# Layer norms taken by token chunk, with the units before and after them reordered chunk by chunk

## The reference

```python
def _layer_norm(x, g, b):
    mu = jnp.mean(xf, axis=-1, keepdims=True)
    var = jnp.mean(jnp.square(xf - mu), axis=-1, keepdims=True)
    return (xf - mu) * lax.rsqrt(var + LN_EPS) * g + b
...
for l in range(DEPTH):
    if l < N_A:
        y, h = _short_conv(x, conv_hist[l], a_w_in[l], a_conv_w[l], a_w_out[l])
    else:
        k_new, v_new, logf_new = _shared_kv(x, kv_w, f_w, f_b)
        cum = lax.cumsum(logf_all, axis=1)
        y = _fox_prompt(...) or _fox_sample(...)
    x = _layer_norm(ALPHA * x + y, ln_g[l, 0], ln_b[l, 0])
    x = _layer_norm(ALPHA * x + _swiglu(x, ffn_w_gu[l], ffn_w_down[l]), ln_g[l, 1], ln_b[l, 1])
```

## Time and profile before

| what | us |
|---|---|
| median of 3 runs (lowest, highest) | 2905.06 (2899.21, 2907.32) |
| the profiled execution | 2906.83 |
| its span, first to last instruction | 2905.2 |
| PE busy | 2696.3 |
| DVE, ACT, POOL busy | 1109.6, 784.1, 951.4 |
| granted PE clock, mean | 0.955 |

### The profile page before, as it was taken

One profiled execution on the slowest core, in us unless ns is written; L12 is line 12 of the kernel. 1 busy time (PEld: TensorE's weight loads), 2 busy tenths in 40 slices (PEclk: granted clock), 3 DMA queues, 4 the chain that ended last, 5 costly groups with the idle time before them and its releaser, 6 DMA issues.

```text
span 2905.2 us, 44679 instructions
## 1 busy us (share of the span) xinstructions
PE 2696.3 (93%) x16907; PEld 2605.1 (90%) x16907; DVE 1109.6 (38%) x2082; ACT 784.1 (27%) x1431; POOL 951.4 (33%) x546
## 2 busy tenths in 40 slices
PE   8999969999999999689997899889799999999994
PEld 8999959999999999579996778779599999999993
DVE  3222362422222222762354555552642222222237
ACT  2111134111111111252223555551511111111114
POOL 2212143112111122352323878843512212112114
PEclk9999969999999999899998989989899999999997
DMA  3111101111111111024688555631011111111111
GB/s 111 44 51 43 45 22 37 47 49 44 45 44 44 53 50 44 23 80 144 197 286 270 143 168 152 179 111 44 22 44 52 44 52 45 44 52 45 44 37 59
DMA packets 203054, 225.87 MB, mean 78 GB/s; under 512 B 13223, under 2 KB 168871, under 8 KB 201884
## 3 DMA queue, kind: packets, MB, share of 16 engines
q1 hardware_dynamic: 194748, 190.40, 21.5%
q0 software_dynamic: 8160, 33.30, 3.7%
HBM read 182.43 MB, written 41.26 MB: 77 GB/s over the span
## 4 chain that ended last, share of the span: by engine, by line
PE 79%; DVE 7%; POOL 4%; issue 4%; DMA 3%; ACT 2%; SPq 1%; POOLq 0%; DVEq 0%; ACTq 0%
PE ps L1746 24%; PE ps L1747 24%; PE ps L1748 24%; POOL ss L830 2%; PE ps L2012 2%; DVE ln_t L1405 1%; DVE ln_t L1409 1%; PE ps L2042 1%; DVE ln_d L1350 1%; PE ps L1997 1%; PE ps L1994 1%; DMA ncb<-ccum 1%; DMA o_t<-oe 1%; PE ps L2029 1%; PE ps L2028 1%
## 5 line engine op out<-in xcount | busy, mean ns | idle before, releaser
L1746 PE MATMUL ps<-xh,whi 128*128 128x344 f32 x3288 | 1068.0, 325 | 31.5 <-POOL xl L711 18.4
L1747 PE MATMUL ps<-xl,whi 128*128 128x344 f32 x3288 | 1055.2, 321 | 0.0
L1748 PE MATMUL ps<-xh,wlo 128*128 128x344 f32 x3288 | 1055.0, 321 | 0.0
L664 POOL TENSOR_TENSOR wlo<-wraw,whi 128x1024 fp32r<-128x1024 f32 x197 | 471.2, 2397 | 1659.0 <-ACT whi L890 1658.9
L1746 PEld LDWEIGHTS ps<-xh,whi 128*128 128x128 f32 x3288 | 620.7, 189 | 59.5 <-POOL xl L711 34.6
L1748 PEld LDWEIGHTS ps<-xh,wlo 128*128 128x128 f32 x3288 | 622.3, 189 | 0.0
L1747 PEld LDWEIGHTS ps<-xl,whi 128*128 128x128 f32 x3288 | 622.1, 189 | 0.0
L890 ACT ACTIVATE whi<-wraw 128x1024 fp32r<-128x1024 f32 x197 | 208.2, 1058 | 1116.9 <-DMA wraw<-ffn_w_gu 649.3
L1746 PE MATMUL ps<-zh,whi 128*128 128x344 f32 x1440 | 465.7, 323 | 17.6 <-DVE x L1477 9.4
L1747 PE MATMUL ps<-zl,whi 128*128 128x344 f32 x1440 | 464.1, 322 | 0.0
L1748 PE MATMUL ps<-zh,wlo 128*128 128x344 f32 x1440 | 462.1, 321 | 0.0
(11 more groups left out here) (209 smaller groups left out, 2384.3 us busy)
## 6 DMA issues: line engine op xcount, KB each, us to landing
wraw<-ffn_w_gu SPq DMA_DIRECT2D x88, 512.0 KB, 3.9
wraw<-ffn_w_down SPq DMA_DIRECT2D x44, 512.0 KB, 3.5
kp<-cache_k SPq DMA_DIRECT2D x32, 512.0 KB, 5.5
vp<-cache_v SPq DMA_DIRECT2D x32, 512.0 KB, 4.1
wraw<-a_w_in SPq DMA_DIRECT2D x24, 512.0 KB, 3.7
wraw<-kv_w SPq DMA_DIRECT2D x16, 512.0 KB, 4.3
q_t<-hl POOLq DMA_DIRECT2D x8, 1024.0 KB, 4.6
v_t<-vst POOLq DMA_DIRECT2D x8, 1024.0 KB, 6.9
```

The lines of the kernel that those rows point to most:

```text
L664: pool.tensor_tensor(narrow(wlo[:, s, :], cols), narrow(wraw[:, s, :], cols), f32(narrow(whi[:, s, :], cols)), ALU.subtract).then_inc(w_lo, 1)
L1746: pe.matmul(out, w_h, m_h, start=start, stop=False)
L1747: pe.matmul(out, w_h, m_l, start=False, stop=False)
L1748: return pe.matmul(out, w_l, m_h, start=False, stop=stop)
```

## The change

The norm is split into steps for one chunk each (`ln_block_mean`, `ln_spread`, `ln_rstd`, `ln_scale` on DVE; `ln_square_sum`, `ln_mean`, `ln_root`, `ln_out` on ACT; `ln_mean`, `ln_var`, `ln_bc` on PE; `ln_low` and `ln_sum` with a chunk on POOL), and the units around it are reordered. The last three of the 8 out- or o-units (`CUT` = 5) run as a `triple`: chunk by chunk, in each chunk the three units, each unit now with a PSUM bank of its own. The first three units behind norms 0 and 2 (gate, up, gate of the FFN) are a triple too, and so are `f`, the first v-unit and the first q-unit behind norm 1. The last group of the down-projection goes over its 24 pieces chunk by chunk. PE's matmuls of the norm are placed between the chunks. The first v-unit's weights get a fourth place (`xraw`, `xhi`, `xlo`). Behind norm 1, ACT takes the chunks of v and q before it starts the decay chain, and DVE takes f and the low part of q likewise. At the end, output rows 0 and 1 are made inside norm 3, and of the last chunk POOL makes three blocks and DVE five. Buffers of the norm move, `ln_mu` becomes two chunks, and the variances go to columns 400 on of a bank that is in use otherwise. The number of matmuls stays the same.

```diff
+CUT = 5
...
+class Pieces:
...
+    def __init__(self, whole, by_chunk):
+        order = [(m, None) for m in whole if m] + [(m, c) for c in range(NCH) for m in by_chunk if m]
+        self.taken = {p: i + 1 for i, p in enumerate(order)}
...
+AFTER_PROJ = Pieces(range(CUT), range(CUT, KB))
+AFTER_DOWN = Pieces((), range(KB))
+LN_PIECES = (AFTER_PROJ, AFTER_DOWN) * DEPTH
+LN_MEAN = ((3, 4, 5), (0, 0, 7)) * DEPTH
+LN_VAR = ((6, 6, 6), (1, 1, 7)) * DEPTH
+LN_BC = ((3, 4, 5), (2, 3, 6)) * DEPTH
+VCOL = 400
...
-                for q in range(4):
-                    gate_up(n0 + q - q % 2, n0 + q - q % 2, q // 2, q % 2, used(g0 + q))
+                for q in range(3):
+                    gate_up(n0 + q - q % 2, n0 + q - q % 2, q // 2, q % 2, (full[q], g0))
+                gate_up(n0 + 2, n0 + 2, 1, 1, (full[0], g0 + 3))
...
             def proj_low(stage, i):
-                for m in range(KB):
-                    low(SLOTS[stage] + m + WR, SLOTS[stage] + m + WR)
-                    if i == 2 and m >= 1:
+                n = SLOTS[stage]
+                for m in range(CUT):
+                    low(n + m + WR, n + m + WR)
+                    if i == 2 and m >= 2:
                         ln_sum(i, m)
-                    if i == 0 and m >= 6:
-                        ln_sum(i, m - 4)
                 if i == 0:
-                    for m in range(4, KB):
+                    for m in range(2, CUT):
                         ln_sum(i, m)
-                ln_low(i)
...
+                for c in range(2):
+                    for m in range(CUT, KB):
+                        ln_sum(i, m, c)
+                ln_sum(i, 5, 2)
+                ln_low(i, 0, 0, 2)
+                ln_sum(i, 6, 2)
+                ln_low(i, 0, 2, 5)
+                low(n + KB, n + KB)
+                ln_sum(i, 7, 2)
+                ln_low(i, 0, 5, 8)
+                low(n + KB + 1, n + KB + 1)
+                low(n + KB + 2, n + KB + 2)
+                for c in range(1, NCH):
+                    ln_low(i, c, 0, KB)
...
                 n0, g0 = SLOTS[stage], UNITS[stage]
-                for m in range(KB):
+                for m in range(CUT):
                     high(n0 + m + WR, n0 + m + WR, (full[2], g0 + m + 1))
                     if i == 2 and m >= 1:
                         ln_squares(i, m)
-                    if i == 0 and m >= 4:
-                        ln_squares(i, m - 3)
                 if i == 0:
-                    for m in range(5, KB):
+                    for m in range(1, CUT):
                         ln_squares(i, m)
+                n, freed = n0 + KB, g0 + KB
+                for m in range(CUT, KB):
+                    ln_squares(i, m, 0)
+                ln_square_sum(i, 0)
+                ln_squares(i, 5, 1)
+                ln_mean(i, 0)
+                ln_squares(i, 6, 1)
+                ln_root(i, 0)
+                ln_squares(i, 7, 1)
+                ln_square_sum(i, 1)
+                ln_squares(i, 5, 2)
+                ln_mean(i, 1)
+                ln_out(i, 0, 0, 2)
+                ln_squares(i, 6, 2)
+                ln_root(i, 1)
+                ln_out(i, 0, 2, 5)
+                high(n, n, (full[0], freed))
+                ln_squares(i, 7, 2)
+                ln_square_sum(i, 2)
+                ln_out(i, 0, 5, 8)
...
+                first_gate(0)
+                ln_out(i, 1, 0, 3)
+                ln_mean(i, 2)
+                ln_out(i, 1, 3, 5)
+                ln_root(i, 2)
+                ln_out(i, 1, 5, 8)
+                first_hidden(0)
+                second_gate(0)
+                ln_out(i, 2, 0, 4)
+                first_gate(1)
+                ln_out(i, 2, 4, 8)
+                first_hidden(1)
+                second_gate(1)
+                first_gate(2)
+                high(n0 + 3, n0 + 3, (full[0], g0 + 3))
+                first_hidden(2)
+                high(n0 + 4, n0 + 4, (full[1], g0 + 3))
+                second_gate(2)
                 high(n0 + 5, n0 + 5, (full[2], g0 + 3))
...
+            high(n0 + 1, n0 + 1, ffn[0].at("down", FG * KB * NCH))
+            ln_out(1, 1, 0, 4)
+            ln_mean(1, 2)
+            ln_out(1, 1, 4, 8)
+            first_v(0)
+            ln_root(1, 2)
+            first_q(0)
+            ln_out(1, 2, 0, 8)
+            for c in range(1, NCH):
+                first_v(c)
+                first_q(c)
+            act.wait_ge(free[1], UNITS["f"] + NCH)
+            act.activation(scol[:, 0, 0, :], stage[0][:, TP:T], ACT.Copy).then_inc(kv["v"], 1)
+            high(n0 + 2, n0 + 2, (full[0], g0 + 2))
+            act.wait_ge(free[0], UNITS["f"] + NCH)
             act.activation(fe[:, :], fz[:, :], ACT.Abs).then_inc(kv["fa"], 1)
...
+            def ln_spread(i, c):
+                s = ln[i]
+                dve.wait_ge(*s.at("mu", c + 1))
+                dve.tensor_tensor(sl(ln_v, c), sl(ln_mp, c), ln_mu[:, c % 2, :], ALU.subtract).then_inc(s["dev"], 1)
+                dve.wait_ge(*s.at("s2", s.pieces.total(KB - 1, c)))
+                dve.wait_ge(*s.at("m2", c + 1))
+                dve.scalar_tensor_tensor(sl(ln_m2, c), sl(ln_m2, c), -1.0 / KB, sl(ln_s2, c), ALU.mult, ALU.add).then_inc(s["dsum0"], 1)
+                dve.wait_ge(*s.at("dsum0", c + 1))
+                dve.wait_ge(*s.at("v2", c + 1))
+                dve.tensor_tensor(sl(ln_m2, c), sl(ln_m2, c), sl(ln_v, c), ALU.add).then_inc(s["dsum"], 1)
...
+            def ln_scale(i, c, blocks):
+                s = ln[i]
+                for k, m in enumerate(blocks):
+                    j = c * KB + (k if i == 3 and c == 2 else m)
                     if j >= 3:
                         dve.wait_ge(*s.at("y", j - 2))
-                    dve.tensor_tensor(ln_t[:, j % 3, :], sl(x32[:, m, :], c), sl(ln_mu, c), ALU.subtract).then_inc(s["t"], 1)
+                    dve.tensor_tensor(ln_t[:, j % 3, :], sl(x32[:, m, :], c), ln_mu[:, c % 2, :], ALU.subtract).then_inc(s["t"], 1)
                     if m == 0:
-                        dve.wait_ge(*s.at("bc", c + 1))
+                        dve.wait_ge(*(s.at("mu", NCH + 1) if i == 3 and c == 2 else s.at("bc", c + 1)))
...
+                def take(m, c):
+                    u = m - CUT
+                    xm = sl(x32[:, m, :], c)
+                    dve.wait_ge(full[u], g0 + CUT + c + 1)
+                    if first:
+                        if m == KB - 1 and c == 0:
+                            dve.wait_ge(stored, 16 * 3)
+                        dve.scalar_tensor_tensor(xm, f32(sl(xh[:, m, :], c)), ALPHA, ps[:, u, 0:CH],
+                                                 ALU.mult, ALU.add).then_inc(free[u], 1)
+                        dve.wait_ge(free[u], g0 + CUT + c + 1)
+                        dve.scalar_tensor_tensor(xm, f32(sl(xl[:, m, :], c)), ALPHA, xm,
+                                                 ALU.mult, ALU.add).then_inc(s["r"], 1)
+                        ln_diff(i, m, c, s.at("r", NCH * CUT + (KB - CUT) * c + u + 1))
+                    else:
+                        dve.tensor_tensor(xm, xm, ps[:, u, 0:CH], ALU.add).then_inc(free[u], 1)
+                        ln_diff(i, m, c, (free[u], g0 + CUT + c + 1))
+                for m in range(CUT, KB):
+                    take(m, 0)
+                ln_block_mean(i, 0)
+                take(5, 1)
+                ln_spread(i, 0)
+                take(6, 1)
+                ln_rstd(i, 0)
+                take(7, 1)
+                ln_block_mean(i, 1)
+                take(5, 2)
+                ln_spread(i, 1)
+                ln_scale(i, 0, range(0, 2))
+                take(6, 2)
+                ln_rstd(i, 1)
+                ln_scale(i, 0, range(2, 5))
+                take(7, 2)
+                ln_block_mean(i, 2)
+                ln_scale(i, 0, range(5, 8))
             proj("out", 0, True)
-            ln_finish(0)
...
+                def last_down(grp):
...
+                    def take(c, a, b):
+                        for m in range(a, b):
+                            j = c * KB + m
+                            down_sum(grp, m, c, j)
+                            if m >= 1:
+                                ln_diff(i, m, c, s.at("sum", DBANKS + grp * KB * NCH + j + 1))
+                    take(0, 0, 8)
+                    ln_block_mean(i, 0)
+                    take(1, 0, 3)
+                    ln_spread(i, 0)
+                    take(1, 3, 5)
+                    ln_rstd(i, 0)
+                    take(1, 5, 8)
+                    ln_block_mean(i, 1)
+                    take(2, 0, 1)
+                    ln_scale(i, 0, range(0, 2))
+                    take(2, 1, 2)
+                    ln_scale(i, 0, range(2, 4))
+                    take(2, 2, 3)
+                    ln_spread(i, 1)
+                    ln_scale(i, 0, range(4, 6))
+                    take(2, 3, 4)
+                    ln_scale(i, 0, range(6, 8))
+                    take(2, 4, 5)
+                    ln_rstd(i, 1)
+                    take(2, 5, 8)
```

(79 more changed lines are left out.)

578 lines of the change are left out of this document (344 added, 234 removed).

## The result

| | median us (lowest, highest) | ratio to before, 95% interval |
|---|---|---|
| before | 2904.6 (2899.21, 2914.52) | |
| changed | 2892.01 (2884.33, 2896.27) | 0.995 [0.9938, 0.9961] |

What follows compares the result with a forecast made beforehand. The prediction took PE's matmuls plus its waits as the bound, paced around the norms by DVE with POOL. Gains at norms 0, 1, 2, 3 less clock, 33.6 + 11 + 23 + 4.4 - 9 = 63, gave 2842 us, range 2795 to 2880.

Steps and rivals of the forecast that it cites:

- The signs on PE's stops: Norms 0 and 2: no PE idle row over 10 us; first FFN unit: PE waits 5 to 9 us for chunk 0's blocks.
- the differences 3 and 4 at t = 14: Norm 0, counted from 353.07: DVE's whole-width differences 3 and 4 with their sums end at 14, between 12 and 16.5.
- 18 us, plus 1.5: Norm 0: DVE's remaining list behind (2, 5) takes 18 us, plus 1.5 for POOL's weight part; chunk 0 out at about 54.
- DVE's next chunk needs 12.5 to 15.5 and its last 10.3, both inside that: Norm 0 behind chunk 0: DVE's work for the later chunks fits inside PE's 36 us.
- 11 to 12 us a chunk: Norm 1, last down-projection: DVE's pace for pieces of 1.53 to 1.9 us; third block mean about 52.5 us after first sum.
- the decay chain: Behind norm 1: chain of 21 us starts after the last q chunk; PE waits some 10 us, next unit 26.2 after the triple.
- my lower bounds: Lowest gains: 20 us at norm 0, 12 at norm 2, 0 at norm 1 and -6 at norm 3.
- I charged 3 us at three norms: Norms 0, 1 and 2: cost of half-clock matmuls after PE's wait, each 24 costing 3.8 us more; 0 to 20 in all.
- Rival B: DVE as the bound throughout: lower bounds, 26 to 40 us gained, 2865 to 2880; chance 0.2.
- rival A: Placement fits: differences not held by the lock, chain hidden behind a unit; upper bounds, 2790 to 2820; chance 0.22.
- Rival C: Slower through PE's clock: short waits keep it at 0.50 through the triples; eight triple units make 2933; chance 0.05.
- D: No effect: DVE's same in-order chain only moves and PE waits elsewhere as long; 2897 to 2913; chance 0.03.

Runs made afterwards that it cites:

- e1: Against the changed kernel, POOL's sums of squares cut to 8 columns per chunk at all four norms (variances wrong): 2873.0 us, 0.9874 of before.
- e2: Against the changed kernel, chunk 1's broadcast and chunk 2's mean moved inside the first FFN chunk at norms 0 and 2: 2886.1 us, 0.9933 of before.
- e13: Against the changed kernel, low parts of the first three FFN units' weights written by ACT instead of POOL at norms 0 and 2: 2892.0 us, 0.9949 of before.
- e11: Against the changed kernel, four more 344-column DVE operations behind each block mean of each norm: 2922.3 us, 1.0047 of before.
- e9: Against the changed kernel, 42 added matmuls ahead of PE's waits for the first FFN unit's weights at norms 0 and 2: 2893.6 us, 0.9956 of before.
- e5: Against the changed kernel, DVE takes chunk 0 of unit 5 ahead of differences 3 and 4 at norm 0: 2892.4 us, 0.9952 of before.
- e6: Against the changed kernel, chunk 1's variances at norms 1 and 3 put into PSUM bank 7 instead of bank 1: 2892.3 us, 0.9952 of before.
- e14: Against the changed kernel, POOL's sums cut to 8 columns, chunk 1's broadcast earlier and three weights' low parts on ACT, together: 2862.7 us, 0.9842 of before.
- e10: Against the changed kernel, POOL's sums cut to 8 columns and the normalised blocks' low parts written by ACT as copies: 2874.5 us, 0.9892 of before.
- e15: Against the changed kernel, the square root's table loaded ahead by an added root one square earlier in ACT's order: 2890.2 us, 0.9941 of before.
- e8_fill: Against the changed kernel, 56 added matmuls behind the wait for weights, just ahead of the first FFN chunk of norms 0 and 2: 2918.2 us, 1.0049 of before.

## Why the prediction was wrong

**Right.** Gains come from norms 0 and 2. POOL holds DVE. PE waits for `hl`. Half clock came behind PE's longer waits (rows of 0.49 us for 0.32 behind those of 5.29, 1.93, 10.85 and 3.23 us at norm 0). The signs on PE's stops came out half: I had said none over 10 us and 5 to 9 for chunk 0's blocks, and the one at norm 0 is 10.85 (20.90 before); at norm 2 it is 9.65, where the longest before was 5.48.

**Norm 0, DVE's way to chunk 0.** I set the differences 3 and 4 at t = 14, between 12 and 16.5, "nearer to rows 3"; they ended at 16.4. The fault is in the choice: rows 3 show a difference beside a POOL sum that began earlier, here each of the two sums was met by a new POOL instruction of 3.2 to 3.4 us, and the first difference by a weight part. e1 has them done at 12.2. Next, "18 us, plus 1.5" for the lock from the end of (chunk 2, unit 5) to chunk 0's last block: measured 24.6 for the same list, with the step on unit 7 at 5.6 us instead of 2 and the one on unit 6 at 3.4. In that stretch I charged the hold once, for the weight part, and not for POOL's low parts and sums, which stand in the same stretch because the change puts them there. Last, I let the chunk be out with DVE's last operation; ACT's and POOL's part of the last block take 2.5 us more, at norm 2 as well. Together 2.4 + 5.1 + 2.5, and 3.5 for PE's waits, half clock and norm matmuls up to (chunk 2, unit 5), which ended at 39.9 and not at 34: the blocks were out 13 us late. Norm 2 is alike: (chunk 2, unit 5) ended at 27.8 for my 28.2, but DVE's last block of chunk 0 at 50.7 for 46.3, with 2.5 more behind it.

**Norm 0 and 2, behind chunk 0.** The step "DVE's next chunk needs 12.5 to 15.5 and its last 10.3, both inside that" failed: 42 us passed instead of 36, with PE waits of 3.23 and 0.55. I had treated PE's 36 us as free running, but DVE restarts only with a broadcast behind the first FFN chunk, and beside two weight parts. e2 prices the first at 1 to 2 us at norm 0 and 1 at norm 2, e13 all three weight parts, one of which lies ahead of chunk 0's last blocks, at 2.4 and 2.1.

**Norm 1.** The price of a piece was given as 1.53 free and up to 1.9, and I put "11 to 12 us a chunk". The third block mean came 63.8 us after the first sum for my 52.5. The held differences are 7.9 us of this, and I had looked for their hold in POOL's sums alone: the low parts of chunk 0 and a weight part, which the change puts there, held five of the 21 for longer than any sum. Without POOL's sums (e1) the mean is at 56.4. The triple then took 39.9 us from this mean to its end, in e1 as well, where I had 33.5; PE's waits of 2.86 and 1.40 us and its half-rate rows lie in it. What won some back is the decay chain, which was as described and cheaper than sized: 5.42 us of waiting for some 10, and kvq3 22.6 us behind the triple, not 26.2. DVE is through the chain at 1286.5, 18.8 us after ACT's first step, not 21.

**Norm 3.** The same sum failed by less: third mean at 55.5 for 52, with 3.7 us of held differences, the last block 79.0 us after the first sum for 74, and the end of the last copy at 86.4 for 78.2. The output rows behind the last block took 7.4 us; I had 4.2, for four rows at the pace of DVE's copies alone. So at norms 1 and 3 my lower bounds (0 and -6) were nearer than my values, and the one of norm 1 was a little optimistic. Both sums stood on an engine that e11 shows to be the bound, and its work had grown even without a hold: three free pieces are 4.6 us of DVE, three adds with one whole-width difference and sum 3.8 (1.35 and twice 1.23).

**Clock.** I charged 3 us at three norms. Counted in the timelines by rows over 0.46 us, 57 big matmuls of norm 0 are slow (58 before), 89 of norm 1 (31 before) and 25 of norm 2 (11 before), in the changed kernel nearly all at the 0.49 us of the 1.2 GHz level. Each costs 0.13 us more (0.29 from one to the next for 0.16), so 24 cost 3.1 us and not the 3.8 that I took, and norm 1 has 7.5 us more of it than before. e9 shows that those of the first FFN chunk cost nothing. Whether the others do was not tried.

**The choice among the cases.** Rival B, DVE as the bound throughout, is what happened; e11 shows it, and e5 and e6 agree. I gave it 0.2 with 26 to 40 us of gain. Its price failed too: I built the lower bound of each norm from one hold (the differences at norm 0, the piece at norm 1), while every chunk has its own holds, and took sums as independent of where POOL's work had been moved. Forecast and rival A rested on DVE being inside PE's time after chunk 0; nothing in the profile of before showed this, as DVE was busy for 69 to 88% of the stretches behind the mean while executing the same work undivided. Rival C's mechanism shows at norm 1 (0.84 in the granted clock) but not its price; D (2897 to 2913) was near in size and wrong in mechanism, for the norms did move: two shorter, one longer, and norm 1 longer by no more than its scatter.

**Open.** In e14 norm 0 is 5.8 us and norm 2 4.0 us above the forecast. POOL's low parts (4.3 us earlier mean in e10) and the last block's latency are the candidates; no run isolates them. Norm 1 keeps 4.1 us above the forecast in e1: the mean at 56.4 for 52.5, with its five held differences, and the longer triple stand against the cheaper chain, and how much of the triple is half clock no run tells. e15's first root shows that a wait taken from DVE doesn't always come back, so e11's one for one holds for work added, and not in full for waits removed.

## What to carry to other kernels

When work is interleaved so that one engine fills another's waits, add up the in-order list of the engine that feeds it, over all chunks, at the price that it has beside the neighbours that the change gives it; if that list is as long as the stretch, the stretch will not shrink below it. Test for it by adding a few idle operations to the suspected engine: a cost of one for one says more than any wait in the trace. Here the change paid at norms 0 and 2, and lost at norm 3 and, within its scatter, at norm 1, where DVE already took 24.5 of 30.1 us. That cutting a step in three is free only on an engine with slack fits this, but no run tries it alone. And count the holds in the order that the change makes: POOL's low parts stood beside DVE's pieces only because the norm was moved there.

## What the runs showed of the hardware that was not expected

A block of 56 matmuls ahead of a loop made the loop slower. In e8_fill the loop of FFN 0, whose code is unchanged, took 15 us more than in the changed kernel. The waits of PE with no releaser, first in that stretch of e8_fill, then in the changed kernel (us in total, times, longest):

```profile
PE ps L2069 <- issue: 11.5, 8, 3.2
```

```profile
PE ps L2069 <- issue: 3.7, 4, 1.2
```

The stretch itself, in e8_fill and in the changed kernel:

```profile
473.00:1182.49 709.49, 696.14 (x4368) 693.57 (x4367) 192.29 (x390) 118.36 (x184) 145.70 (x61) 0.99 0.15 45
```

```profile
467.13:1161.21 694.08, 688.56 (x4369) 687.09 (x4367) 192.24 (x390) 118.12 (x184) 145.99 (x61) 1.00 0.16 46
```

Eight waits instead of four make 7.8 us, and PE is busy for 7.6 us longer with the same work, at a granted clock of 0.99 for 1.00. No run here shows the cause. It isn't simply the number of instructions ahead: with 42 matmuls at the same place, e9_fill_first has 695.4 us for this loop, and FFN 1's loop in e8_fill, with both blocks of 56 ahead of it, 694.4, with four waits and 4.1 us in all. It warns that an edit can move the time of a stage with unchanged code by more than most of the effects above; the stretches are what to compare.
